# First value blocks of the decode attention loaded ahead of the keys, and the second norm's scaling and low parts redistributed over three engines

## The reference

```
h = rms_norm(x, norm_mlp) * (1 + sc2) + sh2           # the second norm, modulated
return x + g2 * (square(relu(h @ w_up)) @ w_down)      # the MLP

# sample attention, 8 sequences, 4096 cached keys each, per head:
logits = q . k + bias                                  # keys of 3 chosen blocks of 256 and the own block
out = softmax(logits) @ v                              # values gathered through the page table
```

## Time and profile before

| | |
|---|---|
| median of 3 runs | 897.68 us (897.31 to 902.81) |
| profiled execution | 903.88 us, its span 902.0 us |
| mean granted TensorE clock | 0.976 |
| PE, PEld busy | 841.3 us (93%), 592.8 us (66%) |
| DVE, ACT, POOL busy | 441.7 us, 338.1 us, 293.3 us |
| moved by DMA | 254.02 MB, mean 282 GB/s |

### The profile page before, as it was taken

How to read it: one execution, slowest core, us unless ns; L and a number is a source line. 1 busy time by engine, 2 the same in 40 slices (tenths; PEclk the granted TensorE clock), 3 DMA queues, 4 the chain that set the end, 5 groups by cost and what they waited for, 6 DMA issues and landing times.

```text
span 902.0 us, 20195 instructions
## 1 busy us (share of the span) xinstructions
PE 841.3 (93%) x7634; PEld 592.8 (66%) x7634; DVE 441.7 (49%) x845; ACT 338.1 (37%) x701; POOL 293.3 (33%) x191
## 2 busy tenths in 40 slices
PE   5899999998999699999999999999999999999664
PEld 4577776666766266666666666666766666677553
DVE  2643222774776965575574564565564332013211
ACT  4133223886124646145145145154154254331110
POOL 0330003956221634244243343343333344440000
PEclk9699999999999699999999999999999999999988
DMA  9942236694999879999999999999999797779995
GB/s 294 326 153 94 94 106 256 194 343 147 323 299 308 284 260 333 303 310 333 304 301 341 300 322 322 298 314 329 301 318 373 247 333 257 235 251 349 399 397 213
DMA packets 167825, 254.02 MB, mean 282 GB/s; under 512 B 10454, under 2 KB 69419, under 8 KB 167755
## 3 DMA queue, kind: packets, MB, share of 16 engines
q1 hardware_dynamic: 166995, 250.66, 81.9%
q0 software_dynamic: 768, 2.51, 0.7%
HBM read 248.56 MB, written 4.75 MB: 281 GB/s over the span
## 4 chain that ended last, share of the span: by engine, by line
PE 82%; DVE 6%; DMA 3%; issue 3%; ACT 3%; SPq 3%; POOL 0%; DVEq 0%; ACTq 0%
PE PS L1523 78%; DMA W<-in_cache_v_dram 2%; SPq L501 2%; DMA mixT<-in_x_prompt_dram 1%; DVE W L1308 1%; DVE xT L1376 1%; PE PS L1872 1%; PE PS L1746 1%; PE PS L2055 1%; DVE mixT L1248 1%; DVE hT L1087 1%; SPq L496 1%; ACT mixT L878 1%; DVE mixT L1245 0%; DVE stat L1250 0%
## 5 line engine op out<-in xcount | busy, mean ns | idle before, releaser
L691 POOL TENSOR_TENSOR W_split<-W,W_split 128x1024 fp32r<-128x1024 f32 x72 | 172.8, 2399 | 289.0 <-ACT W_split L851 133.9
L1523 PE MATMUL PS<-gT_split,W_split 128*128 128x512 f32 x576 | 197.9, 404 | 1.2 <-DVE xT L1376 0.5
L1308 DVE STREAM_TRANSPOSE W<-rwT 128x512 f32<-128x512 f32 x256 | 162.7, 682 | 39.1 <-PE PS L1523 30.5
L1523 PE MATMUL PS<-rwT_split,W_split 128*128 128x512 f32 x512 | 174.9, 405 | 0.0
L1523 PE MATMUL PS<-hT_split,W_split 128*128 128x512 f32 x416 | 162.0, 399 | 0.5 <-ACT mixT L924 0.5
L1523 PEld LDWEIGHTS PS<-gT_split,W_split 128*128 128x128 f32 x576 | 108.1, 188 | 50.5 <-issue 14.8
L1523 PEld LDWEIGHTS PS<-rwT_split,W_split 128*128 128x128 f32 x512 | 97.1, 190 | 34.3 <-issue 14.8
L1523 PE MATMUL PS<-kT_split,W_split 128*128 128x512 f32 x256 | 100.0, 391 | 0.0
L851 ACT ACTIVATE W_split<-W 128x1024 fp32r<-128x1024 f32 x32 | 33.9, 1059 | 168.9 <-DMA W<-in_w_up_dram 168.8
L1376 DVE SCALAR_TENSOR_TENSOR xT<-PS,mods,xT 128x512 f32<-128x512 f32 x64 | 47.3, 742 | 97.0 <-PE PS L1523 96.8
L1523 PEld LDWEIGHTS PS<-hT_split,W_split 128*128 128x128 f32 x416 | 79.3, 191 | 16.7 <-issue 1.6
(11 more groups left out here) (276 smaller groups left out, 966.5 us busy)
## 6 DMA issues: line engine op xcount, KB each, us to landing
rwT<-in_cache_k_dram SPq DMA_DIRECT2D x256, 256.0 KB, 4.2
W<-in_cache_v_dram SPq DMA_DIRECT2D x256, 256.0 KB, 3.9
W<-in_w_ada_dram SPq DMA_DIRECT2D x12, 2048.0 KB, 10.8
W<-in_w_up_dram SPq DMA_DIRECT2D x32, 512.0 KB, 5.6
W<-in_w_down_dram SPq DMA_DIRECT2D x32, 512.0 KB, 5.5
W<-in_w_down_dram SPq DMA_DIRECT2D x5, 2048.0 KB, 17.3
W<-in_w_in_dram SPq DMA_DIRECT2D x3, 2048.0 KB, 7.9
rwT<-in_w_up_dram SPq DMA_DIRECT2D x3, 2048.0 KB, 11.4
```

The lines of the kernel that those rows point to most:

```text
L691: pool.tensor_tensor(rows_part(RAW, q, W_split), rows_part(RAW, q), rows_part(HIGH, q, W_split), ALU.subtract).then_inc(w_low, 1)
L1308: dve.transpose(ktb[u % 2][:, :, g, :], k_ring[:, j % SLOTS, pg, :]).then_inc(kt_ev, 1)
L1523: return pe.matmul(out, lhsT, rhs, start=start, stop=stop, **kw)
```

## The change

Four edits, with the new lines beside the old:

1. SyncE issues the first four value blocks when `ada_part` reaches 11, before it waits for the end of the prompt's attention. They no longer go out behind the last two steps of the output projection.
2. VectorE's norm product takes the modulation's factor with it (`xT * mod_a * rstd`, one SCALAR_TENSOR_TENSOR in place of a TENSOR_TENSOR). ScalarE then only adds the shift.
3. GpSimd makes the low parts of tiles 0 to 4. For tiles 5 to 7 ScalarE makes the high part straight from the unshifted product (shift added on the way), and VectorE makes the low part (`hT + shift - high`) in one SCALAR_TENSOR_TENSOR, after its eighth norm product.
4. TensorE weighs only units 0 and 1 before the first `up` product. Unit 2 goes between the first half of `up(0, 0)` and `score_keys(2, 0)`. Each stage ends with the unit before the one that it had, and the last stage with two, 6 and 7.

```diff
+            sp.wait_ge(ada_part, 11)
+            for j in range(SLOTS):
+                load_values(0, j, True)
             sp.wait_ge(ada_part, 12)
             sp.wait_ge(at_out_ev, HP)
             sp.wait_ge(outs, 16 * 3)
...
                     load_up(0, m - PARTS)
-                if m >= FT - 2:
-                    for j in range(2 * (m - FT + 2), 2 * (m - FT + 2) + 2):
-                        load_values(0, j, True)
...
-            stream_low(h_hi, h2_high, h2_ready)
+            for f in range(POOL_LOWS):
+                pool.wait_ge(h2_high, f + 1)
+                pool.tensor_tensor(h_lo[:, f, :], hT[:, f, :], h_hi[:, f, :], ALU.subtract).then_inc(h2_ready, 1)
...
-                act.activation(hT[:, f, :], hT[:, f, :], ACT.Identity, bias=mods[:, SH2 + f, 0:1],
-                               scale=mod_a[:, 1, f, 0:1]).then_inc(h2_raw, 1)
+                act.activation(hT[:, f, :], hT[:, f, :], ACT.Identity, bias=mods[:, SH2 + f, 0:1]).then_inc(h2_raw, 1)
...
+            for f in range(POOL_LOWS, FT):
+                act.wait_ge(h2_norm, f + 1)
+                act.activation(h_hi[:, f, :], hT[:, f, :], ACT.Identity, bias=mods[:, SH2 + f, 0:1]).then_inc(h2_high, 1)
...
             for f in range(FT):
-                dve.tensor_tensor(hT[:, f, :], xT[:, f, :], rstd[:, :], ALU.mult).then_inc(h2_norm, 1)
+                dve.scalar_tensor_tensor(hT[:, f, :], xT[:, f, :], mod_a[:, 1, f, 0:1], rstd[:, :], ALU.mult, ALU.mult)\
+                   .then_inc(h2_norm, 1)
+            for f in range(POOL_LOWS, FT):
+                dve.wait_ge(h2_high, f + 1)
+                dve.wait_ge(h2_norm, f + 1)
+                dve.scalar_tensor_tensor(h_lo[:, f, :], hT[:, f, :], mods[:, SH2 + f, 0:1], h_hi[:, f, :],
+                                         ALU.add, ALU.subtract).then_inc(h2_low, 1)
             scores_out(1, 0)
             turn_keys(2, 0)
...
                     if starting and m == 0:
-                        pe.wait_ge(h2_ready, k + 1)
+                        pe.wait_ge(h2_ready, k + 1) if k < POOL_LOWS else pe.wait_ge(h2_low, k + 1 - POOL_LOWS)
...
                     up(i + 1, u - 4, 0, 4, opening)
+                    if opening and u == 4:
+                        weigh_values(0, 2)
                     if keys:
                         score_keys(i + 3, u - 4)
                     up(i + 1, u - 4, 4, FT, opening)
-                    weigh_values(i + 1, u)
+                    weigh_values(i + 1, u - opening)
+                    if opening and u == UNITS - 1:
+                        weigh_values(0, u)
...
-            for u in range(4):
-                weigh_values(0, u)
+            weigh_values(0, 0)
+            weigh_values(0, 1)
```

More of the change, by code:

```diff
@@ L325, in decoder_step @@
         up_ps, relu_ev, sqr_ev, dn_ps, dn_ev = sems("up_ps relu_ev sqr_ev dn_ps dn_ev")
-        h2_norm, h2_raw, h2_high, g_high, g_low = sems("h2_norm h2_raw h2_high g_high g_low")
+        h2_norm, h2_raw, h2_high, h2_low, g_high, g_low = sems("h2_norm h2_raw h2_high h2_low g_high g_low")
         w_high, w_low = sems("w_high w_low")
@@ L382, in decoder_step @@
         LAST = DB - 1
+        POOL_LOWS = 5
         ROUNDS = BLOCKS // SLOTS
@@ L623, in chain @@
                 pool.wait_ge(win_step, step[0])
[L625 to L631, removed]
+            for f in range(FT):
+                pool.wait_ge(h_high, f + 1)
+                pool.tensor_tensor(h_lo[:, f, :], hT[:, f, :], first_hi[:, f, :], ALU.subtract).then_inc(h_ready, 1)
             pool.wait_ge(bias_out, 16)
@@ L982, in back, with shifted @@
                 down_high(i + 1, 1)
-            def modulated(f):
+            def shifted(f):
                 act.wait_ge(h2_norm, f + 1)
-                act.activation(hT[:, f, :], hT[:, f, :], ACT.Identity, bias=mods[:, SH2 + f, 0:1],
-                               scale=mod_a[:, 1, f, 0:1]).then_inc(h2_raw, 1)
[L990 to L993, removed]
+                act.activation(hT[:, f, :], hT[:, f, :], ACT.Identity, bias=mods[:, SH2 + f, 0:1]).then_inc(h2_raw, 1)
+            shifted(0)
+            for f in range(POOL_LOWS):
+                if f + 1 < POOL_LOWS:
+                    shifted(f + 1)
                 act.wait_ge(h2_raw, f + 1)
                 act.activation(h_hi[:, f, :], hT[:, f, :], ACT.Copy).then_inc(h2_high, 1)
+            for f in range(POOL_LOWS, FT):
+                act.wait_ge(h2_norm, f + 1)
+                act.activation(h_hi[:, f, :], hT[:, f, :], ACT.Identity, bias=mods[:, SH2 + f, 0:1]).then_inc(h2_high, 1)
             probs_out(0, 1, first=True)
```

## The result

| | median | runs | profiled | span | clock |
|---|---|---|---|---|---|
| before | 901.56 us | 11 (897.31 to 908.07) | 903.88 | 902.0 | 0.976 |
| changed | 907.83 us | 11 (904.14 to 912.16) | 909.59 | 907.8 | 0.978 |

Ratio 1.0072, 95% interval 1.0046 to 1.0097: slower by 6.5 us (4.2 to 8.7). With more runs the median of before rose from the 897.7 that the prediction started from to 901.6. So the forecast of 900.0 missed the median by 7.8 us: 3.9 by its base, and 3.9 by the change (6.3 between the medians, in place of 2.3; the ratio gives 6.5).

The account below looks back on a forecast made before the run. TensorE, 82% of the chain, was taken as the bound, waiting for values before `up(0, 0)`. Terms -2.0 + 2.8 + 1.0 + 0.5 = +2.3 us gave 900.0 us against the median 897.7, range 892.5 to 905.0.

Parts of the forecast that it names:

- Cost: nothing: SyncE's early value loads: eight transfers end at about 212, within its own wait before the keys at 215.5, costing nothing.
- The start of the scores, -2.0: TensorE's `score_keys(2, 0)` starts when VectorE's turned keys are ready, at 314.4 instead of 316.4: -2.0 us.
- The norm product's price: VectorE's norm product with the factor costs the same as the plain 0.69 us, so the eighth ends at 304.8 as before.
- the rival at 906.6: VectorE's product with a factor runs at half rate from two SBUF inputs, 11 operations, 6.6 us more; chance 0.14.
- The low parts: VectorE's three low parts take turns with GpSimd, 3 x 1.68 = 5.0 us, ending at 309.9.
- the rival at 893.4: VectorE's low parts pass freely beside GpSimd, keys ready at 311.1, -4.3 us in sum; chance 0.18.
- The clock, +2.8: TensorE, after standing still 5 us before 314.4, restarts at half clock for 5.2 to 6.2 us: +2.8 us.
- The rival at 897.2: TensorE's clock stays at full, or recovers during the first half of `up(0, 0)`: -0.5 us in sum; chance 0.15.
- One value unit more, +1.0: TensorE has one more value unit behind the norm, 1.06 us less a little overlap: +1.0 us.
- The wait for the next sequence's values, +0.5: Units 6 and 7 together delay the next sequence's value blocks to 355.5, TensorE wants them at 355.1: +0.5 us.
- the fourth rival: SyncE's values stay a step late in the loop, TensorE waits 1 to 2 us in seven sequences, 907 to 914; chance 0.05.

Follow-up runs that it names:

- g1: Kernel before, plus GpSimd waiting for VectorE's ranking to end before its low part of the first `w_up` quarter; timed +0.9 ± 2.6 us against before.
- g3: Changed kernel, plus GpSimd waiting for VectorE's ranking to end before its low part of the first `w_up` quarter; timed +4.6 ± 2.1 us against before.
- e2: Kernel before with edits 2 and 3 alone, loads and value units as before; timed +1.0 ± 2.0 us against before.
- e4: Changed kernel with unit 3 moved beside unit 4 at the first stage's end, units 4 to 7 in their old stages; timed +5.8 ± 2.5 us against before.
- e1: Kernel before with edit 1 alone, units 0 to 3 still ahead of `up(0, 0)`; timed +2.7 ± 1.7 us against before.
- e3: Changed kernel with all eight low parts on GpSimd; timed ratio 1.0083 (1.0052 to 1.0113) against before.
- p1: Second profile of the unaltered kernel before; 66.57 us from first residual add to unit 0, scores 21.03 us behind unit 0.
- p3: Second profile of the unaltered changed kernel; 68.26 us from first residual add to unit 0, stages +5.8 us against before.
- p4: Third profile of the unaltered changed kernel; 68.33 us from first residual add to unit 0, stages +4.8 us against before.
- e5: Changed kernel with old ring order in the loop, eight low parts on GpSimd, `take_queries(2)` ahead of them; timed -2.2 ± 2.3 us against before.

## Why the prediction was wrong, step by step

**Edit 1, "Cost: nothing".** The cover held:

```profile
205.64 5.51 SPq L502 DMA_DIRECT2D W<-in_cache_v_dram  x8
215.47 13.30 SPq L502 DMA_DIRECT2D rwT<-in_cache_k_dram  x16
```

The eight transfers end before 212, and the keys go out at 215.47, as at 215.54 before. But the sum began at unit 0 and took everything ahead of it as unchanged ("unit 0 and the own keys end at 295.4 as before"). **This is the step that failed**: a term put at nothing. The stage ahead took 66.55 before and 68.9 in the mean of three changed profiles, +2.3 us, all three with the meeting. The earlier trace rows began at the norm, so the low part that lies 0.3 us behind a VectorE instruction was not in what the prediction read. g1 to g3 show that the meeting is what lengthens that stage: behind the gate it takes 66.6 to 66.8, with and without the early loads.

Why the changed kernel meets more often, if it does, is not shown. The first `w_up` quarter is issued 36.0 us after the first residual add and `quadmax` stands 42.9 us after it, in all profiles. ScalarE started on the quarter 5.3 to 6.5 us after its issue, and where that was under 5.7 GpSimd came first wherever no gate stood; at 5.76 and 5.77 it went either way. Without the early loads 1 of 4 ungated profiles met, with them 5 of 7; the mean landing was 6.07 and 5.80 us. That is too few to tell from chance, and e2 met without early loads.

**The start of the scores, -2.0.** The place was right: forecast 21.1 us behind unit 0, measured 21.10, 21.11, 21.11. The terms under it were too: the early transfers, the wait for GpSimd, unit 2 behind the half. What was wrong is what it was held against, since the mean of before is 21.66, not 23.11. Worth -0.6. One reading under it was wrong and did no harm: the row at 309.59, x4, is the second half of the fourth unit, whose first half ran at 307.14, so its 1.92 us are not the price of a whole unit at half clock. Unit 2 took 1.06 at full clock, and TensorE waited for VectorE behind it anyway.

**The norm product's price.** VectorE's eight products and three low parts, to be held against the earlier trace rows:

```profile
300.07 8.46 DVE L1414 SCALAR_TENSOR_TENSOR hT<-xT,mod_a,rstd 128x512 f32<-128x512 f32 x8
308.44 4.90 DVE L1419 SCALAR_TENSOR_TENSOR hT_split<-hT,mods,rwT_split 128x512 fp32r<-128x512 f32 x3
```

Alone one takes 0.746 to 0.752 us, beside GpSimd up to 1.768. So no half rate: the rival at 906.6 is refuted. The rule of the Trainium skill (Vector Engine (DVE) Microarchitecture Reference, "Points that are easy to get wrong") does not hold for this form here: twice the plain product's 0.69 us would be 1.4. That the measured 907.8 lies near this rival's time is chance. The low parts took 4.90 us where 5.0 were forecast, in turns with GpSimd, which refutes the rival at 893.4.

**The clock, +2.8.** These are the stretches after the 6.10 us wait:

```profile
317.50:318.00 0.50, 0.22 (x5) 0.20 (x9) 0.50 (x3) 0.00 (x0) 0.00 (x0) 0.50 0.65 90
321.00:321.50 0.50, 0.50 (x2) 0.33 (x1) 0.50 (x2) 0.00 (x0) 0.00 (x0) 0.50 0.00 0
322.50:323.00 0.50, 0.50 (x4) 0.42 (x3) 0.38 (x1) 0.00 (x0) 0.00 (x0) 1.00 0.00 0
```

The 1.2 GHz level was granted from about 315.4, within the wait, to about 322, 4 us of work, where 5.2 to 6.2 were forecast. From scores to `gsum` it took 6.6 us in the mean against 4.95: +1.6. The rival at 897.2 had two roads. The clock did recover during the first half, at about 308.2; but the wait took it away again, so its price, no loss at the scores, is refuted.

**One value unit more, +1.0**: the double unit took 2.29, 1.92 and 1.93 us in the three profiles against 1.07 for one, +1.0 in the mean.

**The wait for the next sequence's values, +0.5**, was inside its bound of 2.5 but mis-sized, and the road to it was incomplete. SyncE kept the forecast pace:

```profile
350.25 0.85 SPq L502 DMA_DIRECT2D W<-in_cache_v_dram  x2
351.78 0.85 SPq L502 DMA_DIRECT2D rwT<-in_cache_k_dram  x2
353.31 0.85 SPq L502 DMA_DIRECT2D W<-in_cache_v_dram  x2
```

The second block's last transfer was issued by 354.16, some 4.0 us after unit 6 (forecast 4.1). But the unit's second half started at 359.52, 5.4 us later, against the 3.9 taken from the earlier trace rows, a median of all 256. From the unit's start to the loop's first residual add it is 5.15 us against 2.97 before: +2.2. Of this the wait itself is 1.15. The other 1.05 is the price of the split, since each half of a unit takes as long as a whole one; the prediction had no such term. The other two profiles say the same: waits of 1.31 and 0.32 us, and +2.35 and +1.35. In the mean that is +2.0, a wait of 0.9 and a half unit of 1.05. e4 takes this away. With the double unit it makes 3.4 in this profile and +2.9 in the mean of three (`gsum` to the loop's add, 37.3 against 34.38). The wait doesn't return in the loop: from 365 to 880 us TensorE waits 0.6 us in all for values, 0.9 before. So the fourth rival is refuted.

**The sum.** Forecast -2.0 + 2.8 + 1.0 + 0.5 = +2.3. Measured in the means of three profiles: +2.3 ahead, -0.6, +1.6, +2.9 behind, together +6.3, against the 6.5 timed. The 4 us between the two sums are +2.3 for the stage ahead, +1.4 for the start of the scores, -1.2 for the clock and +1.4 behind. That 6.3 and 6.5 agree so closely is partly luck: what lies outside these stages differed by +1.5 and -2.3 us.

**The base.** 897.68 us was the median of three runs, and eleven gave 901.56. With that base the same sum would have said 903.9, and the range, moved up with it, would have reached 908.9 and held the measured 907.83. So the range was missed by the base as much as by the terms above: the two are of one size, 3.9 us each.

**What stays open.** e1 and e3 were timed 4 and 6 us above their stages. Both profiles were without a meeting; runs with one would add 1.5 to 3.9 us, which could cover most of e1's gap if nearly all of them met, and not all of e3's. Whether early loads make a quarter land sooner isn't shown either, and no run has edit 4 without edit 2.

## What to carry to other kernels

Lay before and after beside each other from well ahead of the first edited instruction, at events that both have. A stage that no edit touches can still take longer, and an instruction of 0.23 us can be what sets the residual add when it starts just behind a long one of GpSimd's. Where two lists come within 0.3 us of each other, take both orders into the range. And take a second profile of the kernel before a term is read off as the difference from it: the scores started 23.11 us behind unit 0 in the execution that the forecast used, and 21.03 and 20.85 in two others. Ask of each row whether it is a whole unit of work or a part, since here a part costs as much as the whole.

## What the runs showed of the hardware that was not expected

- A VectorE TENSOR_SCALAR of 128x4 took 0.23 us when it started 0.08 us or more ahead of a GpSimd operation of 2.4 us (p1: 268.38 against 268.46), and 2.05 to 2.46 when it started up to 0.4 us behind it, or 0.03 ahead of it (p3: 270.16 against 270.19). In all six it ended 0.02 to 0.04 us after GpSimd's: the price was GpSimd's remaining time.
- Two blocks of values weighed in one go took 1.06 us, and each of them 1.05 when a wait stood between them (changed: 357.32 and 359.52).
- After waits of 1.48 to 1.66 us TensorE went on at full clock (e2, p3, p4), after waits of 1.76 to 2.17 us at the same place it was granted 1.2 GHz for some 3 to 4 us (changed, e4, e5). Six executions don't show what decides it.
- One wait more in GpSimd's list, for a semaphore that VectorE raises at about that time anyway, cost nothing that the runs can tell (g1: ratio 1.0010, interval 0.9982 to 1.0039).
- The start on a load of 512 KB came 5.3 to 6.5 us after its issue, and 5.77 to 6.31 in three executions of one kernel. Since the rest stands still to 0.1 us, this decides which engine comes first.
